# Expert tokens fetched by indirect DMAs from a DRAM copy, and first level operands made beside the gate projections

## The reference

```
def _gla_scan(q, k, log_f, v, s0):            # a gated scan over chunks, per head and direction
    ...
        decay = jnp.exp(jnp.where(causal[:, :, None], diff, -jnp.inf))
        scores = jnp.sum(qc[:, :, :, None, :] * kc[:, :, None, :, :] * decay, axis=-1)
...
def _expert_choice_ffn(h, w_router, w_gate, w_up, w_down):
    cap = EC_CAPACITY_FACTOR * t // N_EXPERTS                     # 64 of 512 tokens, 32 of 256 context tokens
    aff = jax.nn.softmax(jnp.einsum('btd,de->bte', h, w_router).astype(jnp.float32), axis=-1)
    vals, idx = lax.top_k(aff.transpose(0, 2, 1), cap)
    xg = jax.vmap(lambda hb, ib: hb[ib])(h, idx)
    hid = jax.nn.silu(jnp.einsum('becd,edf->becf', xg, w_gate)) * jnp.einsum('becd,edf->becf', xg, w_up)
    out = jnp.einsum('becf,efd->becd', hid, w_down) * vals[..., None].astype(h.dtype)
    return jax.vmap(lambda ob, ib: jnp.zeros((t, d), h.dtype).at[ib.reshape(-1)].add(ob.reshape(-1, d)))(out, idx)
```

## Time and profile before

| what | value |
|---|---|
| median of three runs | 3815.66 us (3811.54 to 3823.98) |
| the profiled execution: its own time, its span | 3824.45 us, 3821.3 us |
| PE matmul busy | 3581.4 us (94%) |
| DVE, ACT, POOL busy | 1179.8, 911.5, 142.1 us |
| granted TensorE clock, mean over the span | 0.968 |
| read from HBM, written | 404.51 MB, 2.10 MB |
| chain that ended last | PE 86%, DVE 8%, ACT 2% |

### The profile page before, as it was taken

How to read it: one execution, slowest core, us unless ns; L and a number is a source line. 1 busy time by engine, 2 the same in 40 slices (tenths; PEclk the granted TensorE clock), 3 DMA queues, 4 the chain that set the end, 5 groups by cost and what they waited for, 6 DMA issues and landing times.

```text
span 3821.3 us, 46294 instructions
## 1 busy us (share of the span) xinstructions
PE 3581.4 (94%) x19542; PEld 2060.3 (54%) x19542; DVE 1179.8 (31%) x2497; ACT 911.5 (24%) x1715; POOL 142.1 (4%) x162
## 2 busy tenths in 40 slices
PE   8999999999999899999999788899999999787999
PEld 4465455654555555655657566454434656664543
DVE  1323550022323540023433685300002333762011
ACT  1343130111243220124324220211113234211110
POOL 0000000000000000000000340000000000320000
PEclk9999999999999899999999899899999999888999
DMA  4111172312111262202010001157752110012997
GB/s 146 60 51 50 60 277 88 105 45 66 56 50 56 86 245 94 94 25 106 28 34 28 1 1 56 66 206 299 272 209 95 39 42 19 1 50 105 357 341 275
DMA packets 113099, 409.60 MB, mean 107 GB/s; under 512 B 12288, under 2 KB 14464, under 8 KB 112512
## 3 DMA queue, kind: packets, MB, share of 16 engines
q1 hardware_dynamic: 112896, 406.66, 29.4%
HBM read 404.51 MB, written 2.10 MB: 106 GB/s over the span
## 4 chain that ended last, share of the span: by engine, by line
PE 86%; DVE 8%; ACT 2%; issue 1%; DMA 1%; POOL 0%; DVEq 0%; SPq 0%; ACTq 0%
PE bank L1518 84%; PE bank L1633 1%; DMA ring<-in_stream 1%; DVE work L1307 1%; DVE h_sb L2193 0%; ACT work L1880 0%; DVE ring L1281 0%; DVE work L2036 0%; DVE work L2038 0%; DVE levels L1307 0%; DVE work L1377 0%; PE bank L1705 0%; DVE cpad L1271 0%; DVE small L1376 0%; DVE ring L1280 0%
## 5 line engine op out<-in xcount | busy, mean ns | idle before, releaser
L1518 PE MATMUL bank<-h_sb,ring 128*128 128x512 f32 (+2 forms) x3200 | 1251.2, 548 | 25.1 <-ACT h_sb L920 13.4
L1518 PEld LDWEIGHTS bank<-h_sb,ring 128*128 128x128 f32 (+1 forms) x3200 | 594.2, 191 | 570.0 <-issue 529.3
L1518 PE MATMUL bank<-y_sb,ring 128*128 128x512 f32 (+1 forms) x1152 | 474.9, 574 | 9.7 <-DVEq L199 9.7
L1518 PE MATMUL bank<-work 128*128 128x128 f32 (+7 forms) x3168 | 426.2, 322 | 29.8 <-DVE small L2043 12.2
L1518 PEld LDWEIGHTS bank<-work 128*128 128x128 f32 (+2 forms) x3168 | 317.5, 180 | 123.4 <-issue 85.9
L1518 PEld LDWEIGHTS bank<-y_sb,ring 128*128 128x128 f32 x1152 | 219.8, 192 | 259.8 <-issue 245.1
L1840 ACT ACTIVATE work<-bank 128x512 f32<-128x512 f32 (+1 forms) x262 | 132.6, 520 | 798.2 <-PE bank L1518 647.2
L1518 PE MATMUL bank<-ring,h_sb 128*128 128x128 f32 (+2 forms) x2144 | 283.1, 310 | 1.4 <-ACT work L1033 0.7
L1518 PEld LDWEIGHTS bank<-ring,h_sb 128*128 128x128 f32 (+2 forms) x2144 | 231.9, 185 | 43.7 <-issue 40.9
L1518 PE MATMUL bank<-ring,work 128*64 128x512 f32 (+1 forms) x800 | 209.4, 596 | 0.5 <-DMA ring<-in_stream 0.5
L1518 PE MATMUL bank<-y_sb,work 128*64 128x128 f32 (+2 forms) x920 | 168.7, 431 | 0.0
(11 more groups left out here) (286 smaller groups left out, 3461.7 us busy)
## 6 DMA issues: line engine op xcount, KB each, us to landing
ring<-in_stream SPq DMA_DIRECT2D x578, 512.0 KB, 4.6
y_sb<-in_stream SPq DMA_DIRECT2D x110, 512.0 KB, 6.3
h_sb<-in_stream SPq DMA_DIRECT2D x40, 512.0 KB, 8.1
work<-in_stream SPq DMA_DIRECT2D x20, 512.0 KB, 9.0
work<-in_bias SPq DMA_DIRECT2D x2, 2688.0 KB, 9.1
x_sb<-in_xT SPq DMA_DIRECT2D x4, 512.0 KB, 6.7
out<-x_sb SPq DMA_DIRECT2D x8, 256.0 KB, 2.0
const<-in_consts SPq DMA_DIRECT2D x1, 1085.0 KB, 15.8
```

Of the source, the lines that this page charges most:

```text
L1518: return nc.tensor.matmul(o, a, b, start=first, stop=last, skip_group_check=True)
```

## The change

**Gather.** As ACT evacuates a turned tile it tells POOL, which stores the tile to a DRAM tensor `tokens` (768 x 1024) by a plain DMA; six stores in layer 0, four in layer 1. For each quad PE now multiplies the one-hots with a column of token numbers (`slot_tokens`, 10 or 8 matmuls with one column each, into bank 6), DVE copies the result as integers to `slot_tok`, and POOL issues one indirect DMA per 128 slots, three in layer 0 and two in layer 1, each fetching 128 rows of 4 KB into `picked` (tiles 1 to 3 of `h_tok`). PE waits for the rows (`rows_in`) and transposes them, 24 or 16 transposes of 128x128 (`turn_rows`), and ACT copies the banks as before. `slot_tokens` of quad q+1 stands ahead of the up pass q, `turn_rows` in it after round r == 2. `weigh` no longer waits for the gather.

**First level operands.** The differences of pass 0 are made on DVE as soon as PE has started the first gate unit (`w_turn`), ACT's exponentials stand ahead of the evacuation of that unit, and DVE's products follow them. DVE no longer waits for the evacuation of all units. For this the operands of even passes lie in ring slots that the three gate units don't use, and in `rstd`; the seventh level of odd passes goes into the ring, so one of the next stage's eight units (the sixth) waits for the last pass's last read. POOL clears the sums of the first direction early, those of the second once the inputs are read.

```diff
-        level_sets = [[ring[:, n * ALL:(n + 1) * ALL] for n in range(7)],
-                      [h_sb[:, n * ALL:(n + 1) * ALL] for n in range(6)] + [rstd[:, :]]]
+        def level_sets(l):
+            early, late = ring_blocks(l)
+            in_ring = lambda at: ring[:, at:at + ALL]
+            return [[in_ring(at) for at in early] + [rstd[:, :]],
+                    [h_sb[:, n * ALL:(n + 1) * ALL] for n in range(6)] + [in_ring(late[0])]]
...
                     if phase == "out2":
-                        sp.wait_ge(levels_read, 6 * l + 5)
+                        sp.wait_ge(levels_read, 6 * l + (6 if places[unit][0] in last_level_slots(l) else 5))
...
                     if slot in INPUT_ROOM:
-                        sp.wait_ge(tokens_turned, 1)
+                        sp.wait_ge(tokens_turned, 6 + 4)
...
-                def gather():
+                def slot_tokens():
 
                     pe.wait_ge(one_hot_ready, me.nth(one_hot_ready))
-                    for n in range(6 if both else 4):
+                    claim(6, "dve")
+                    for n in range(2 + both):
+                        for j in range(4 if n < 2 else 2):
+                            of = one_hot[:, j, n * P:(n + 1) * P] if n < 2 else one_hot_c[:, j, :]
+                            ins = mm(banks[6][:, n:n + 1], of, cst(C_TOKEN + j + (0 if n < 2 else 4), 1), j == 0,
+                                     j == (3 if n < 2 else 1))
+                    ins.then_inc(full_for_dve, 1)
+
+                def turn_rows():
+
+                    at["rows"] = at.get("rows", 0) + 1
+                    pe.wait_ge(rows_in, 16 * rows_until(both, at["rows"]))
+                    for n in range(2 * (2 + both)):
                         b = 6 + n % 2
                         claim(b, "act")
                         for k in range(4):
                             ks = slice((4 * (n % 2) + k) * P, (4 * (n % 2) + k + 1) * P)
-                            o = banks[b][:, k * P:(k + 1) * P]
-                            if n < 4:
-                                pair = slice(n // 2 * 2 * CAP, (n // 2 + 1) * 2 * CAP)
-                                for j in range(4):
-                                    ins = mm(o, h_tok[:, j, ks], one_hot[:, j, pair], j == 0, j == 3)
-                            else:
-                                for j in range(2):
-                                    ins = mm(o, h_tok[:, 4 + j, ks], one_hot_c[:, j, :], j == 0, j == 1)
+                            ins = nc.tensor.transpose(banks[b][:, k * P:(k + 1) * P], picked[:, n // 2, ks], ident)
                         ins.then_inc(full_for_act, 1)
...
                     def next_gather(r):
-                        if r == 1:
-                            at["gathered"] = gather()
+                        if r == 2:
+                            at["gathered"] = turn_rows()
...
+                    if more:
+                        slot_tokens()
                     expert_pass(("up", q), expert_input(q), 4, "dve", next_gather if more else None)
...
                 for n in range(15):
                     b = (n % 2) * 2
+                    if n == 15 - GATE_UNITS:
+                        exponentials(l, 0)
...
-                me.notify(act_output)
                 me.notify(inputs_read)
...
                 me.notify(gates_ready)
-                await_(act_output)
...
+                dve.wait_ge(w_turn, first_gate[l] + 1)
                 me.link(key_difference(V, 0), act_input, wait=False)
...
-                await_(gather_read)
...
+                def chosen_tokens():
+                    bank_full()
+                    me.link(V.tensor_copy(slot_tok[:, 0:2 + both], banks[6][:, 0:2 + both]), freed_by_dve)
+                    me.notify(slots_ready)
...
+                n_tok = 6 if need_ctx(l) else 4
+                for j in range(n_tok):
+                    pool.wait_ge(tokens_turned, 6 * l + j + 1)
+                    V.dma_start(tokens[j * P:(j + 1) * P, :], h_tok[:, j, :]).then_inc(tokens_stored, 16)
+                pool.wait_ge(tokens_stored, 16 * (6 * l + n_tok))
+                for q in range(N_QUADS):
+                    pool.wait_ge(slots_ready, N_QUADS * l + q + 1)
+                    if q:
+                        pool.wait_ge(gather_read, N_QUADS * l + q)
+                    for n in range(2 + need_ctx(l)):
+                        V.indirect_dma_start(picked[:, n, :], None, tokens, bass.IndirectOffsetOnAxis(slot_tok[:, n:n + 1], 0)
+                                             ).then_inc(rows_in, 16)
```

More of the change, by code:

```diff
@@ L78, in build @@
         acc_o = sb("acc_o", ALL)
+        slot_tok = ctx.enter_context(nc.sbuf_tensor("slot_tok", [P, 4], mybir.dt.uint32))
+        tokens = nc.dram_tensor("tokens", (ALL, D_MODEL), f32).ap()
         banks = [ctx.enter_context(nc.psum_tensor(f"bank{i}", [P, 512], f32)) for i in range(8)]
@@ L272, in mem_units, with ring_blocks, head_norm_at, last_level_slots @@
                                dest=[y[:, 2 * hh + j, :] for j in range(2)])
+        GATE_UNITS = 3
+        first_gate = [sum(UNITS[p] for _, m, p in ORDER[:ORDER.index((2, l, "hgrn")) + 1]) - GATE_UNITS for l in range(DEPTH)]
+        def ring_blocks(l):
+            gate_slots = {places[first_gate[l] + n][0] for n in range(GATE_UNITS)}
+            early, late = [], []
+            for of, blocks in ((False, early), (True, late)):
+                at = 0
+                while at + ALL <= RING * 1024:
+                    slots = range(at // 1024, (at + ALL - 1) // 1024 + 1)
+                    wrong = [n for n in slots if (n in gate_slots) != of]
+                    if wrong:
+                        at = (wrong[-1] + 1) * 1024
+                    else:
+                        blocks.append(at)
+                        at += ALL
+            return early[:6], late[:3]
+        def level_sets(l):
[3 more added lines that the diff above has]
+                    [h_sb[:, n * ALL:(n + 1) * ALL] for n in range(6)] + [in_ring(late[0])]]
+        def head_norm_at(l):
+            late = ring_blocks(l)[1]
+            return [[ring[:, at:at + ALL] for at in late[1:]]] * 2 + [level_sets(l)[1][0:2]]
+        def last_level_slots(l):
+            at = ring_blocks(l)[1][0]
+            return range(at // 1024, (at + ALL - 1) // 1024 + 1)
         @block.sync
@@ L491, in build, with rows_until @@
         h_tok = tiles(0, 6, D_MODEL)
+        picked = h_tok[:, 1:4, :]
+        def rows_until(both, q):
+            return 3 * q if both else 3 * N_QUADS + 2 * q
         QUAD = 4
@@ L1002, in hgrn @@
                     if i + 1 < len(PASSES):
-                        exponentials(i + 1)
+                        exponentials(l, i + 1)
                 await_input()
@@ L1018, in experts @@
                     evacuate(h_tok[:, j, g * 512:(g + 1) * 512], banks[4 + n % 4][:, :])
-                if not both:
-                    me.notify(tokens_turned)
+                    if g:
+                        act.wait_ge(freed_by_act, me.done["freed_by_act"])
+                        me.notify(tokens_turned)
                 def gathered_out(q):
@@ L1425, in experts @@
                 for q in range(N_QUADS):
+                    if q + 1 < N_QUADS:
+                        chosen_tokens()
                     for _ in range(3):
```

61 lines of the change are left out of this document (34 added, 27 removed).

## The result

The changed kernel takes **3735.29 us** (median of four runs, 3733.50 to 3737.78) against 3819.62 us for the kernel before (four runs, 3811.54 to 3823.98): a ratio of 0.978, 95% interval 0.9767 to 0.9794. The forecast was 3738 with a range of 3716 to 3796. The profiled execution has a span of 3734.2 us, against 3821.3 before: 87.1 us less.

The account below looks back on a forecast made before the run. PE, with 86% of the chain, was taken as the bound, the weight stream next; 21.1 (operands) + 34.4 + 22.0 (later gathers) + 0.7 (first gathers) = 78.2 us less, from 3815.66 to 3738 us, range 3716 to 3796.

Parts of the forecast that it names:

- First level operands: Start of each layer's scan: operand work moves under the gate units, saving 13.5 us in layer 0, 7.6 in layer 1.
- B1: Layer 1 stretch from the first states to the first gather; forecast gain 0 us.
- Later gathers: Expert up passes: fetch and transposes replace gather matmuls in three quads per layer, saving 34.4 and 29.0 us before stream loss.
- How long a fetch takes: Gather DMAs per quad: taken as 10 us in layer 0 and 8 in layer 1, between bounds 3.8/2.6 and 25/17.
- one after another: Rival: each fetch DMA runs in turn and bounds the kernel; slower from 9.4 us per DMA, 3868 at 12; chance 0.07.
- fetches a little late: Rival: POOL needs 6 us per fetch DMA, so rows arrive late in the gathers; 59.5 us saved, 3756 us; chance 0.15.
- First gathers: Uncovered gather ahead of each layer's first up pass: 0.9 us lost in layer 0, 1.6 won in layer 1, together 0.7.
- What the stream takes back: Layer 1's expert stage: the weight stream takes back 7 of the 29.0 us, 22 stay; layer 0 gives nothing back.
- Waits of PE on `in_stream`, 5 to 10 us in all: Sign in layer 1's gate and down passes, with stream windows near 409 GB/s.
- bound at 370: Rival: layer 1's stream stays under 370 GB/s with rows mixed in; 56 to 60 us stay, 3758 us; chance 0.12.
- The operands' gain: Rival at the scan's pass 0: DVE's masked copying holds it, early operands win nothing; 57 us stay, 3759 us; chance 0.08.
- B: Layer 0 stretch from the first level products to the first gather; forecast gain 0 us.

Follow-up runs that it names:

- the half stream: Changed kernel with each layer 1 expert weight unit loaded by half, PE's instructions untouched: 3729.80 us; the same cut in the kernel before: 3820.68 us, ratio 1.000.
- a semaphore for each: Changed kernel with a separate semaphore for each of a quad's three (layer 1: two) fetches, so PE turns the first 128 rows once there: 3737.35 us.
- the other fills and the row semaphores: Changed kernel with constant-tile transposes in PE's waits in the scan and first gathers, plus a semaphore per fetch: 3712.84 us, ratio 0.9716 to the kernel before.
- the scan's part: Only the early first level operands kept, the old one-hot gather put back, against the kernel before: 3800.09 us, ratio 0.995.

## Why the prediction was right, point by point

- **First level operands: right.** 13.5 and 7.6 us forecast, 14.5 and 7.8 measured, and alone they win 19.0 us. What I had missed for layer 0 is that PE keeps its high clock when it doesn't wait: the first products run at full speed, which I had only as the low end of the range. In layer 1 a wait of 2.88 us stays, and the clock is at 0.50 for the 20 us behind it. B1 is 1.3 us longer, which is within its spread (261.0 to 270.1), so no loss is shown. The rows behind the 7.6 us add up to 7.7.
- **Later gathers: right.** 34.4 us for layer 0, 33.6 measured. The transposes took 3.8 us (4.3 forecast) and the slot matmuls 2.39 (2.3). The cover of three rounds held.
- **How long a fetch takes:** 10 and 8 us taken between bounds that were far apart, with 0.5 more for the copy; 9.2 and 7.8 us measured from the last slot matmul to the rows, copy included, bare. POOL's part is small and the DMAs overlap: three issued within 3.9 us (2464.88 to 2468.76) are there after 8.1. The case "one after another" with 9.4 us per DMA was out of reach. But I had not asked what the loaded fetch takes, on which the later quads rest: 9.5 to 13.3 us in layer 0 and 10.0 to 11.4 in layer 1, against the 16.3 and 10.4 us of the cover. The forecast's "fetches a little late" was nearer than 0.15 says in layer 1, and far in layer 0.
- **First gathers:** 0.7 us forecast for both, 3.4 measured; in layer 0 the fetch with its copy took 9.2 and not 10.5 us, the transposes 4.95 and not 5.5, in layer 1 the fetch 7.8 and not 8.5.
- **What the stream takes back: right in place and size.** 7 us forecast, 6.7 shown by the half stream. "Waits of PE on `in_stream`, 5 to 10 us in all" was the wrong sign to look for: they are 3.7, and another 2.2 us are in PE's busy time.
- **Rivals.** The stream held 408 to 410 GB/s with rows mixed in, so it was not bound at 370. The operands' gain is shown by its own run.
- **The sum** was 78.2 us; the table has 81.4 for the same stretches, and the medians 84.3 (the kernel before was measured at 3819.62 this time, 4 us over the median that I started from). That 3735 came so near to 3738 is in part luck: 6.1 us more were won than the sum says, and 4.0 of them were made up by the slower start. Of the 3.2 us that the stretches won beyond the sum, 2.7 are in the first gathers, where the fetch was priced too high. The largest miss elsewhere, 1.7 us in B, is within that stretch's spread.
- The Trainium skill (DMA: Bandwidth & Descriptors, Anatomy of one DMA) gives 2.0 us and the bytes at 436 GB/s for a DMA of this queue; an estimate by it is 3.2 us for one fetch. The run with a semaphore for each shows the first rows 4.7 us after their issue (2476.13 to 2480.80), with two more under way: the trace does not agree. For all three the estimate was 5.6 us (4.4 and not 4.5 under my term), and they took 8.1.

## What to carry to other kernels

Price a fetch twice, bare and beside the load that will run with it, and set the loaded price against the cover, round by round: here one round less cost 11 us and two less 47. When an engine is relieved in a stage that streams its weights, work out first when the stream would end by itself, the new rows' bytes included; the half stream, with PE's instructions untouched, then measures in one run what it takes back. And where PE waits often for a few microseconds, look at the granted clock behind the waits: filling them won about as much (11.8 us in the scan alone, 22.5 us with the other fills and the row semaphores) as the early operands did (19.0).

## What the hardware showed that I had not expected

- An indirect DMA of 128 rows of 4 KB keeps POOL for 0.93 to 0.97 us (1.36 to 1.42 the first of a layer), the next starts 1.24 us after it, and rows of three are there 8.1 us after the first issue on idle DMA engines. Beside the stream three took 9.5 to 13.3 us in layer 0 (rows and stream together at 332 to 384 GB/s meanwhile) and two 10.0 to 11.4 us in layer 1 (410 GB/s).
- The scan's stretches B and B1 vary between executions and kernels with the same instructions on PE, 334.0 to 340.4 and 261.0 to 270.1 us. The granted clock falls to 0.50 behind some of the short waits and not behind others, and which ones it is differs. With the waits filled B1 was 253.0 and 252.2. The spread of B has the same cause: where B took 334.1, 338.2 and 340.4 us (the changed kernel, the scan's part, a semaphore for each fetch), PE is busy for 287.8, 293.1 and 294.5 us with the same records but for one, at mean clocks of 0.94, 0.92 and 0.92, and it is idle for 45 to 46 us in each. Of B1 this explains the low end (261.0 us at 0.90, against 266.5 at 0.85); the 270.1 us were at 0.85 as well, and what sets them apart stays open.
